# Expert steps: four turns of the gated product, in one block or among the next step's first gate products

## The chip, the cores and the metric

The kernel runs on one core of one Trainium2 chip. The metric is the device time of one execution in microseconds, the median of three runs. The times in the profile are those of one profiled execution of the same program.

## The reference

A decoder trunk of two layers on 256 tokens of width 1024, in float32. Each layer has an input projection, a windowed attention group beside a convolution group, an output projection and a feed-forward part. The feed-forward part of the first layer is dense; that of the second is a mixture of 8 experts, two for each token. The change touches the second alone:

```python
def moe_swiglu(h, w_router, w_gate, w_up, w_down):
    ...
    for e in range(N_EXPERTS):
        y = (jax.nn.silu(t @ w_gate[e]) * (t @ w_up[e])) @ w_down[e]
        out = out + combine[:, e:e + 1].astype(t.dtype) * y
    return out.reshape(B, S, D)
```

`w_gate[e]` and `w_up[e]` are 1024 x 3584, `w_down[e]` is 3584 x 1024.

## The kernel before

Every large product is made of three: each operand is split into a high part in the matmul's format and a low part (the rest), and high x high, high x low and low x high are added up in PSUM (`TERMS`, the helper `terms`). For the weights ScalarE (ACT) makes the high part (`high`, L726) and VectorE (DVE) the low part (`low`, L1035). A weight slot is 128 x 2048 values, 1 MB. The raw slots form a ring of 6, the split ones a ring of 3 (`PART_RING`), so ACT may start on a slot only when TensorE has used the slot three before it (`w_used`), and SyncE loads a raw slot when DVE is done with the slot six before it (`w_low_done`).

Each expert takes up to 128 gathered rows of tokens, and its 3584 inner columns go in 7 steps of 512: 56 steps in all (`EG` = 7). A step has six weight slots and 72 products, each with a 128 x 128 stationary operand and 512 moving columns:

- gate: 2 slots, 24 products into PSUM bank 0. Stationary is a piece of the expert's tokens (`xg`, in the profile `hT_both`), moving is the weight (`w_high` or `w_low`);
- up: 2 slots, 24 products into bank 1;
- down: 2 slots, 24 products into banks 4 and 5, stationary is the gated product's split transpose (`act_both`).

Between up and down the step's numbers go round: ACT takes silu of bank 0 (L935), DVE multiplies it by bank 1 into `prod_t` (L1378, 128 x 512, in the profile `work_a`), TensorE turns `prod_t` in four chunks of 128 columns into bank 2 (`turn_act`, L1772: four transposes against the identity, each a weight load and a 128-column matmul), ACT copies bank 2 as the high part (`act_copy`, L917), and DVE makes the low part (`act_low`, L1345).

TensorE's order is written out by hand in `expert_steps`. In round k it does gate and up of step k+1, then down of step k, then the four turns of step k+1. So a block of four turns stands between the last down product of one round and the first gate product of the next. The waits are written beside: `prod_done` ahead of the turns; `silu_done`, `prod_done`, once for each expert `xg_low_done`, and `w_low_done` of the first gate slot ahead of the first gate product. The first step is prepared ahead of the loop, with its turns between its successor's gate and up. In round 54 (`mid`) the turns of the last step stand between the two halves of down, and the last round has only down.

Two other kinds of turns stand in the stream. Once for each of the experts but the first, eight of them turn the fetched rows of the next expert (`turn_rows`, L1743) between up and down, into banks 3 and 6; and once, at `LAST_STEP`, two of them (L1823) go into bank 3.

ACT's order in a round, with t for the round's first slot, is `high(t+2)`, `act_copy`, `high(t+3)`, silu, `high(t+4)` and on; DVE's is `low(t+2)`, `act_low`, `low(t+3)` and on. `high(t+3)` waits until TensorE has used slot t, the first gate slot. Neither order is touched by the change.

Of the kernel before, what the change touches and what calls it, by code (L numbers as in the profile page):

```python
# [22 lines left out]
P = 128  # L23
# [7 lines left out]
def hybrid_trunk(nc, x, attn_norm_g, w_in, q_norm_g, k_norm_g, sinks, conv_w, conv_b, conv_ln_g,  # L31
# [43 lines left out]
    def at(i, per, const):  # L75

        return const if i is None else i * per + const

    with ExitStack() as ctx:
        def sb(name, shape, dt=F32):  # L80
            return ctx.enter_context(nc.sbuf_tensor(name, shape, dt))

        def sem(name):
            return ctx.enter_context(nc.semaphore(name))
# [18 lines left out]
        ident = sb("ident", [P, P])  # L103
# [59 lines left out]
        ps = ctx.enter_context(nc.psum_tensor("ps", [P, 8, 512], F32))  # L163
# [49 lines left out]
        prod_t = work_a[:, 2560:3072]  # L213
# [78 lines left out]
        act_turned = sem("act_turned")  # L292
# [1184 lines left out]
        def _(pe):  # L1477
            def mm(out_, lhsT, rhs, start, stop=False):
                return pe.matmul(out_, lhsT, rhs, start=start, stop=stop, skip_group_check=True)  # L1479

            def terms(out_, tokens, tidx, weights, widx, start, stop, weights_move=True):

                for n, (a, w) in enumerate(TERMS):
                    x_ = tokens[a][tidx]
                    w_ = weights[w][widx]
                    lhsT, rhs = (x_, w_) if weights_move else (w_, x_)
                    last = mm(out_, lhsT, rhs, start and n == 0, stop and n == 2)
                return last

            def slot(s, k, i=None, per=0):  # L1490
                pe.wait_ge(w_low_done, at(i, per, s + 1))
                return [part_slot(0, s, k), part_slot(1, s, k)]
# [245 lines left out]
            def turn_rows(i, per, e):  # L1738

                pe.wait_ge(rows_scaled, at(i, per, e))  # L1740
                for j in range(2):
                    for k in range(4):
                        last = pe.transpose(ps[:, (3, 6)[j], k * P:(k + 1) * P], xrows[:, (4 * j + k) * P:(4 * j + k + 1) * P], ident[:, :])  # L1743
                    last.then_inc(gathered, 1)

            def arriving_rows(j, w):

                for a, ns in ((0, range(2)), (1, range(1))):
                    for m in range(4):
                        k = BY_BANK[4 * j + m] - 4 * j  # L1750
                        pe.wait_ge((first_high_done, first_low_done)[a], 4 * j + m + 1)
                        for n in ns:
                            last = mm(ps[:, 0, :], xg[a][:, 4 * j + k, 0, :], w[n][:, k, :], (a, j, m, n) == (0, 0, 0, 0), (a, j, m) == (1, 1, 3))
                return last

            def gate_up(s, r, i, per, arriving=False, ms=range(2)):

                for m in ms:
                    for j in range(2):
                        w = slot(s + 2 * m + j, 4, i, per)  # L1760
                        if arriving and m == 0:
                            last = arriving_rows(j, w)
                            last.then_inc(w_used, 1)
                            continue
                        for k in range(4):
                            last = terms(ps[:, m, :], xg, (slice(None), 4 * j + k, r, slice(None)), w, (slice(None), k, slice(None)),
                                         j == 0 and k == 0, j == 1 and k == 3)
                        last.then_inc(w_used, 1)

            def turn_act():  # L1770
                for f in range(4):
                    last = pe.transpose(ps[:, 2, f * P:(f + 1) * P], prod_t[:, f * P:(f + 1) * P], ident[:, :])  # L1772
                last.then_inc(act_turned, 1)

            def down_and_scatter(t, a):

                def scatter(hf, b, part):

                    return mm(ps[:, 2 * hf + b, :], slot_of[:, b, :], y_part[part][:, hf * 512:(hf + 1) * 512], part == 0, part == 1)

                pe.wait_ge(slot_copied, 1)
                for j in range(2):
                    w = slot(t + j, 2)
                    for hf in range(2):
                        for f in range(2):
                            last = terms(ps[:, 4 + hf, :], a, (slice(None), 2 * j + f, slice(None)), w, (slice(None), f, slice(hf * 512, (hf + 1) * 512)),
                                         False, j == 1 and f == 1)
                        if j == 1:
                            last.then_inc(y_half, 1)
                pe.wait_ge(y_high_done, 1)  # L1790
                scatter(0, 0, 0)
                pe.wait_ge(y_low_done, 1)
                scatter(0, 0, 1).then_inc(scattered, 1)
                scatter(0, 1, 0)
                scatter(0, 1, 1).then_inc(scattered, 1)
                pe.wait_ge(y_high_done, 2)
                for b in range(NB):
                    scatter(1, b, 0)
                n_passes = passes_in_all(pe)
                pe.wait_ge(y_low_done, 2)  # L1800
                for b in range(NB):
                    scatter(1, b, 1).then_inc(scattered, 1)
                pe.sem_inc(w_used, 2)
                pe.sem_inc(y_copied, 1)
                return n_passes

            def expert_steps(s, n, e, experts, following, i, pers):

                per_s, per_n, per_e = pers
                for k in range(experts * EG):  # L1810
                    last_step = k == experts * EG - 1 and not following
                    t = s + 6 * k
                    if not last_step and (i is not None or k):
                        pe.wait_ge(silu_done, at(i, per_n, DG + n + k + 1))
                        pe.wait_ge(prod_done, at(i, per_n, DG + n + k + 1))
                        nxt = (k + 1) // EG
                        if k % EG == EG - 1:
                            pe.wait_ge(xg_low_done, at(i, 2 * per_e, 2 * (e + nxt + 1)))
                        gate_up(t, (e + nxt) % 2, i, per_s)
                        if i is None and k == LAST_STEP:  # L1820
                            pe.wait_ge(last_onehot, NB)
                            for b in range(NB):
                                last = pe.transpose(ps[:, 3, b * P:(b + 1) * P], onehot[:, b, NE - 1], ident[:, :])  # L1823
                            last.then_inc(slot_turned, 1)
                        if k % EG == GATHER_AT and (k // EG + 1 < experts or following):
                            turn_rows(i, per_e, e + k // EG + 1)
                    pe.wait_ge(act_low_done, at(i, per_n, DG + n + k + 1))
                    if k % EG == 0:
                        pe.wait_ge(y_copied, at(i, per_e, e + k // EG + 1))
                    a = [p_[:, k % 2, :].rearrange("p (f c) -> p f c", f=4) for p_ in act_part]  # L1830
                    if last_step and i is None:
                        return down_and_scatter(t, a)
                    mid = i is None and k == experts * EG - 2
                    for j in range(2):
                        w = slot(t + (0 if last_step else 4) + j, 2, i, per_s)
                        if j == 1 and mid:
                            pe.wait_ge(prod_done, at(i, per_n, DG + n + k + 2))
                            turn_act()
                        for f in range(2):
                            for hf in range(2):  # L1840
                                last = terms(ps[:, 4 + hf, :], a, (slice(None), 2 * j + f, slice(None)), w, (slice(None), f, slice(hf * 512, (hf + 1) * 512)),
                                             k % EG == 0 and j == 0 and f == 0, k % EG == EG - 1 and j == 1 and f == 1)
                        last.then_inc(w_used, 1)
                    if not last_step and not mid:
                        pe.wait_ge(prod_done, at(i, per_n, DG + n + k + 2))
                        turn_act()

# [60 lines left out]
            for k in range(4, KC):  # L1908
                last = mm(ps[:, 5, 0:NE], hT_plain[:, k, P:S], wr[:, k, 0:NE], False, k == KC - 1)
# [59 lines left out]
```

## Time and profile before

| | |
|---|---|
| median of 3 runs | 1340.37 us (1339.83 to 1340.76) |
| span of the profiled execution | 1339.4 us, granted TensorE clock 1.000 |
| TensorE matmul busy | 1330.6 us, 99% of the span |
| weight loads (beside the matmuls) | 1109.6 us, 83% |
| VectorE busy | 1126.6 us, 84% |
| ScalarE busy | 933.0 us, 70% |
| expert steps | 399.7 us to the end of the span, 56 steps |

The span runs from the first to the last instruction of the core; the run's time has 0.97 us more. A matmul's time in the trace reaches past the start of the next one, since matmuls are pipelined. What a matmul costs the stream is the distance of its start to the start of the next, and that is read from the starts in the first column of a timeline.

### The profile page before, as it was taken

The numbers are of one execution on the slowest core, as the hardware profiler recorded it, in microseconds if no ns is written. First come the engines' busy times: TensorE is split into PE (matmuls) and PEld (weight loads), VectorE is DVE, ScalarE is ACT, GpSimd is POOL, SyncE is SP. The second block draws the span as 40 slices with busy tenths as digits, with TensorE's granted clock in tenths as the row PEclk, the third lists the DMA queues.
The fourth block names the chain that finished last, engine by engine and source line by source line (L and its number), as shares of the span: only waits on it lengthen the run. The fifth ranks groups of instructions, "written<-read, shape, count | busy, mean of one in ns | idle before, by whom it ended". The sixth has DMA issues, their size and how long they took to land.

```text
span 1339.4 us, 16909 instructions
## 1 busy us (share of the span) xinstructions
PE 1330.6 (99%) x6957; PEld 1109.6 (83%) x6958; DVE 1126.6 (84%) x818; ACT 933.0 (70%) x787; POOL 130.5 (10%) x143
## 2 busy tenths in 40 slices
PE   9999999999999999999999999999999999999998
PEld 8879888898788888888888888888888888888886
DVE  6867666677678999998998889889888988988997
ACT  6675444465777777777777777777777777777774
POOL 3410000021047500000000000000000000000010
PEclk9999999999999999999999999999999999999999
DMA  9845555646369999999999999999999999999994
GB/s 308 254 160 190 189 190 190 189 154 197 130 214 370 393 390 388 394 358 375 398 382 365 390 393 376 376 387 382 366 394 394 369 374 390 390 366 369 395 395 182
DMA packets 199155, 430.79 MB, mean 322 GB/s; under 512 B 9768, under 2 KB 42816, under 8 KB 199072
## 3 DMA queue, kind: packets, MB, share of 16 engines
q1 hardware_dynamic: 193952, 415.40, 85.7%
q0 software_dynamic: 4576, 13.50, 2.7%
q8 instruction: 57, 0.93, 0.3%
q10 hardware_dynamic: 544, 0.75, 0.2%
q14 instruction: 26, 0.21, 0.0%
HBM read 417.56 MB, written 7.36 MB: 317 GB/s over the span
## 4 chain that ended last, share of the span: by engine, by line
PE 96%; DMA 1%; POOL 1%; DVE 1%; SPq 0%; ACT 0%; issue 0%; DVEq 0%; POOLq 0%
PE ps L1479 92%; PE ps L1772 2%; DMA raw<-in_w_in 1%; POOL work_b L560 1%; PE ps L1743 0%; PE ps L1505 0%; PE ps L1641 0%; DMA work_b<-in_conv_w 0%; DMA hT_both<-hpad 0%; SPq L455 0%; DVE w_low L1035 0%; DVE xr L1339 0%; ACT w_high L726 0%; PE ps L1607 0%; POOL tmp L600 0%
## 5 line engine op out<-in xcount | busy, mean ns | idle before, releaser
L1035 DVE TENSOR_TENSOR w_low<-raw,w_high 128x2048 fp32r<-128x2048 f32 x387 | 892.2, 2306 | 132.9 <-ACT w_high L726 132.5
L726 ACT ACTIVATE w_high<-raw 128x2048 fp32r<-128x2048 f32 x389 | 745.3, 1917 | 267.8 <-PE ps L1479 267.3
L1479 PE MATMUL ps<-w_high,hT_both 128*128 128x512 f32 (+1 forms) x1920 | 599.3, 389 | 0.3 <-DVE w_low L1035 0.3
L1479 PEld LDWEIGHTS ps<-w_high,hT_both 128*128 128x128 f32 x1920 | 358.8, 188 | 71.9 <-DVE w_low L1035 0.8
L1479 PE MATMUL ps<-w_low,hT_both 128*128 128x512 f32 (+1 forms) x960 | 370.7, 386 | 0.0
L1479 PE MATMUL ps<-w_high,act_both 128*128 128x512 f32 x1072 | 342.4, 391 | 0.0
L1479 PEld LDWEIGHTS ps<-w_high,act_both 128*128 128x128 f32 x1072 | 201.4, 188 | 41.5 <-issue 0.3
L1479 PEld LDWEIGHTS ps<-w_low,hT_both 128*128 128x128 f32 x960 | 180.7, 188 | 34.8
L1479 PE MATMUL ps<-w_low,act_both 128*128 128x512 f32 x536 | 208.9, 390 | 0.0
L1479 PE MATMUL ps<-hT_both,w_high 128*128 128x256 f32 (+1 forms) x640 | 140.1, 339 | 0.0
L1479 PEld LDWEIGHTS ps<-hT_both,w_high 128*128 128x128 f32 x640 | 108.9, 190 | 11.0 <-DVE hT_both L1048 0.2
L1479 PEld LDWEIGHTS ps<-w_low,act_both 128*128 128x128 f32 x536 | 100.7, 188 | 20.2
L1479 PE MATMUL ps<-hT_both,w_low 128*128 128x256 f32 x480 | 89.9, 283 | 0.0
L1479 PEld LDWEIGHTS ps<-hT_both,w_low 128*128 128x128 f32 x480 | 74.3, 191 | 3.2
L693 POOL DMA_DIRECT2D y_slots<-work_a x7 | 4.1, 591 | 711.3 <-ACT work_a L955 711.3
L935 ACT ACTIVATE work_a<-ps 128x512 f32<-128x512 f32 x55 | 33.0, 599 | 39.7 <-PE ps L1479 39.7
L1345 DVE TENSOR_TENSOR act_both<-ps,act_both 128x512 fp32r<-128x512 f32 x56 | 38.3, 684 | 0.0
L1378 DVE TENSOR_TENSOR work_a<-ps,work_a 128x512 f32<-128x512 f32 x55 | 37.6, 683 | 0.0
L917 ACT ACTIVATE act_both<-ps 128x512 fp32r<-128x512 f32 x56 | 32.4, 579 | 2.4 <-PE ps L1772 2.4
L1772 PEld LDWEIGHTS ps<-ident,work_a 128*128 128x128 f32 x224 | 27.9, 140 | 7.2
L1772 PE MATMUL ps<-ident,work_a 128*128 128x128 f32 x224 | 33.5, 272 | 0.0
L1066 DVE COPY work_a<-ps 128x512 f32<-128x512 f32 x20 | 13.8, 691 | 22.2 <-PE ps L1479 22.2
(276 smaller groups left out, 708.0 us busy)
## 6 DMA issues: line engine op xcount, KB each, us to landing
raw<-in_moe_w_gate SPq DMA_DIRECT2D x112, 1024.0 KB, 7.9
raw<-in_moe_w_up SPq DMA_DIRECT2D x112, 1024.0 KB, 7.7
raw<-in_moe_w_down SPq DMA_DIRECT2D x112, 1024.0 KB, 7.6
raw<-in_w_in SPq DMA_DIRECT2D x13, 1024.0 KB, 5.6
raw<-in_dense_w_gate SPq DMA_DIRECT2D x11, 1024.0 KB, 5.5
raw<-in_dense_w_up SPq DMA_DIRECT2D x11, 1024.0 KB, 5.3
raw<-in_dense_w_down SPq DMA_DIRECT2D x11, 1024.0 KB, 5.0
raw<-in_w_out SPq DMA_DIRECT2D x8, 1024.0 KB, 6.8
```

The lines of the kernel that those rows point to most:

```text
L560: pool.dma_start(tap_rows[CG * i:CG * (i + 1), l, 0:QUAD * n].rearrange("g (j c) -> g j c", j=n), conv_w[l, 4 * i:4 * i + n, :].rearrange( ...
L693: pool.dma_start(y_dram[bass.ds(m * P, P), :], y_sb).then_inc(y_stored, 16)
L726: act.activation(w_part[0][:, s % PART_RING, :], raw[:, s % RAW_RING, :], ACT.Copy).then_inc(w_high_done, 1)
L917: act.activation(act_part[0][:, k % 2, :], ps[:, 2, :], ACT.Copy).then_inc(act_high_done, 1)
L935: act.activation(silu_t, ps[:, 0, :], ACT.Silu).then_inc(silu_done, 1)
L1035: dve.tensor_tensor(w_part[1][:, q, :], raw[:, r, :], w_part[0][:, q, :], ALU.subtract).then_inc(w_low_done, 1)
L1066: link(dve.tensor_copy(whole, parts[:, :, 1, :]))
L1345: dve.tensor_tensor(act_part[1][:, k % 2, :], ps[:, 2, :], act_part[0][:, k % 2, :], ALU.subtract).then_inc(act_low_done, 1)
L1378: dve.tensor_tensor(prod_t, ps[:, 1, :], silu_t, ALU.mult).then_inc(prod_done, 1)
L1479: return pe.matmul(out_, lhsT, rhs, start=start, stop=stop, skip_group_check=True)
L1772: last = pe.transpose(ps[:, 2, f * P:(f + 1) * P], prod_t[:, f * P:(f + 1) * P], ident[:, :])
```

## The change

In each round from the second on (k > 0, outside the overflow passes) the four turns are not done as one block after down. They are done in the next call of `gate_up`: one turn ahead of each of the first four groups of three gate products. The first turn stands where the block's first turn stood; the other three stand 3, 6 and 9 products later. What the turn writes (bank 2) and reads (`prod_t`) is the same. The waits that stood ahead of the first gate product now stand ahead of the first turn. The end of the fourth turn counts `act_turned`, as before. The turns of the first step and those of the last (`mid`) stay as blocks. 54 of the 56 blocks are changed.

```diff
-            def gate_up(s, r, i, per, arriving=False, ms=range(2)):
+            def gate_up(s, r, i, per, arriving=False, ms=range(2), turns=False):
...
                         for k in range(4):
+                            if turns and (m, j) == (0, 0):
+                                turned_chunk = turn_chunk(k)
+                                if k == 3:
+                                    turned_chunk.then_inc(act_turned, 1)
                             last = terms(ps[:, m, :], xg, (slice(None), 4 * j + k, r, slice(None)), w, (slice(None), k, slice(None)),
                                          j == 0 and k == 0, j == 1 and k == 3)
                         last.then_inc(w_used, 1)
 
+            def turn_chunk(f):
+
+                return pe.transpose(ps[:, 2, f * P:(f + 1) * P], prod_t[:, f * P:(f + 1) * P], ident[:, :])
+
             def turn_act():
                 for f in range(4):
-                    last = pe.transpose(ps[:, 2, f * P:(f + 1) * P], prod_t[:, f * P:(f + 1) * P], ident[:, :])
+                    last = turn_chunk(f)
                 last.then_inc(act_turned, 1)
...
-                        gate_up(t, (e + nxt) % 2, i, per_s)
+                        gate_up(t, (e + nxt) % 2, i, per_s, turns=i is None and k > 0)
...
-                    if not last_step and not mid:
+                    if i is not None and not last_step:
                         pe.wait_ge(prod_done, at(i, per_n, DG + n + k + 2))
                         turn_act()
```

TensorE's order at the seam between two rounds, before: the last down products (`act_both`), the block, the first gate products (`hT_both`) of the next step.

```order
L1479 MATMUL ps<-w_low,act_both 128x512
L1479 MATMUL ps<-w_high,act_both 128x512
L1772 MATMUL ps<-ident,work_a 128x128 [waits prod_done]
L1772 MATMUL ps<-ident,work_a 128x128 x3
L1479 MATMUL ps<-w_high,hT_both 128x512 [waits w_low_done,prod_done,silu_done]
L1479 MATMUL ps<-w_low,hT_both 128x512
L1479 MATMUL ps<-w_high,hT_both 128x512 x2
```

The same place in the changed kernel, where the turn has line 1776:

```order
L1479 MATMUL ps<-w_high,act_both 128x512
L1776 MATMUL ps<-ident,work_a 128x128 [waits w_low_done,prod_done,silu_done]
L1479 MATMUL ps<-w_high,hT_both 128x512
L1479 MATMUL ps<-w_low,hT_both 128x512
L1479 MATMUL ps<-w_high,hT_both 128x512
L1776 MATMUL ps<-ident,work_a 128x128
L1479 MATMUL ps<-w_high,hT_both 128x512
L1479 MATMUL ps<-w_low,hT_both 128x512
L1479 MATMUL ps<-w_high,hT_both 128x512
L1776 MATMUL ps<-ident,work_a 128x128
```

Three turns moved down by 3, 6 and 9 products, and the first gate product's waits moved up onto the first turn. The number of matmuls and of weight loads is the same. On ACT, DVE, SyncE and GpSimd nothing moved.

## Rows read from the trace of the kernel before

**Rows 1.** The page: busy time of the engines; the chain that ended last, by engine.
```profile
PE 1330.6 (99%) x6957; PEld 1109.6 (83%) x6958; DVE 1126.6 (84%) x818; ACT 933.0 (70%) x787; POOL 130.5 (10%) x143
...
PE 96%; DMA 1%; POOL 1%; DVE 1%; SPq 0%; ACT 0%; issue 0%; DVEq 0%; POOLq 0%
```

**Rows 2.** Waits of TensorE, then SyncE, from 400 us: total, times, longest.
```profile
PE ps L1479 <- DVE hT_both L1333: 0.8, 1, 0.8
```
```profile
SPq L415 <- DVE w_low L1035: 787.2, 323, 3.7
```

**Rows 3.** TensorE's timeline in the last down: start, length, engine, line, count.
```profile
1324.44 0.39 PE L1479 MATMUL ps<-w_low,act_both 128*128 128x512 f32 x1
...
1330.56 0.39 PE L1479 MATMUL ps<-w_low,act_both 128*128 128x512 f32 x1
```

**Rows 4.** TensorE's timeline at a block of four turns.
```profile
749.78 0.39 PE L1479 MATMUL ps<-w_high,act_both 128*128 128x512 f32 x1
750.01 0.60 PE L1772 MATMUL ps<-ident,work_a 128*128 128x128 f32 x4
...
750.68 0.39 PE L1479 MATMUL ps<-w_low,hT_both 128*128 128x512 f32 x1
...
751.38 0.39 PE L1479 MATMUL ps<-w_low,hT_both 128*128 128x512 f32 x1
...
753.44 0.39 PE L1479 MATMUL ps<-w_low,hT_both 128*128 128x512 f32 x1
```

**Rows 5.** Chain that ended last: start and length of the products between blocks.
```profile
733.82 16.36 PE ps L1479 x72
750.61 16.37 PE ps L1479 x72
767.42 16.36 PE ps L1479 x72
...
818.75 16.37 PE ps L1479 x72
```

**Rows 6.** TensorE's timeline at the block of two turns.
```profile
1234.99 0.39 PE L1479 MATMUL ps<-w_low,hT_both 128*128 128x512 f32 x1
...
1235.44 0.38 PE L1823 MATMUL ps<-ident,work_b 128*128 128x128 f32 x2
...
1237.26 0.39 PE L1479 MATMUL ps<-w_low,act_both 128*128 128x512 f32 x1
```

**Rows 7.** TensorE's timeline, last row ahead of and a later one behind eight turns.
```profile
455.79 0.39 PE L1479 MATMUL ps<-w_low,hT_both 128*128 128x512 f32 x1
...
458.05 0.39 PE L1479 MATMUL ps<-w_low,act_both 128*128 128x512 f32 x1
```

**Rows 8.** The page's costliest groups: the turn's matmul, with its mean length.
```profile
L1772 PE MATMUL ps<-ident,work_a 128*128 128x128 f32 x224 | 33.5, 272 | 0.0
```

**Rows 9.** Weight loads' timeline: the first two behind the block of 766.82 us.
```profile
767.15 0.19 PEld L1479 LDWEIGHTS ps<-w_high,hT_both 128*128 128x128 f32 x1
767.26 0.19 PEld L1479 LDWEIGHTS ps<-w_low,hT_both 128*128 128x128 f32 x1
```

**Rows 10.** TensorE's timeline: products of 256 columns, then of 512.
```profile
199.36 1.11 PE L1479 MATMUL ps<-hT_both,w_low 128*128 128x256 f32 x8
200.32 2.00 PE L1479 MATMUL ps<-hT_both,w_high 128*128 128x512 f32 x8
```

**Rows 11.** ScalarE's timeline after the block at 766.82 us.
```profile
768.90 0.58 ACT L917 ACTIVATE act_both<-ps 128x512 fp32r<-128x512 f32 x1
770.27 1.92 ACT L726 ACTIVATE w_high<-raw 128x2048 fp32r<-128x2048 f32 x1 [0.79 <-PE ps L1479]
```

**Rows 12.** VectorE's timeline: act_low and low(t+3) of that round; then at 815 us.
```profile
771.24 0.68 DVE L1345 TENSOR_TENSOR act_both<-ps,act_both 128x512 fp32r<-128x512 f32 x1
772.22 2.29 DVE L1035 TENSOR_TENSOR w_low<-raw,w_high 128x2048 fp32r<-128x2048 f32 x1 [0.30 <-ACT w_high L726]
```
```profile
815.33 4.59 DVE L1035 TENSOR_TENSOR w_low<-raw,w_high 128x2048 fp32r<-128x2048 f32 x2
```

## The prediction

> **What bounds the kernel now.** First the page: TensorE is busy for 99% of the span, at a mean granted clock of 1.000 (the table above), and the chain that ended last is 96% TensorE [rows 1]. Then the waits: from 400 us on TensorE waits once, for 0.8 us, in the last step [rows 2]. So in the expert steps the time is the sum of the distances from one matmul's start to the next, and nothing else; a change pays or costs there only by what it does to these distances, or by bringing in a wait. The other engines wait for TensorE: SyncE spends 787.2 us until DVE gives a slot back, and ACT in turn stands idle until TensorE has used a slot [rows 2, 11].
>
> Then the timeline of TensorE, for the price of each kind. From 1324.44 to 1330.56 us, in undisturbed products, there are 27 of them: 6.12 / 27 = **0.2267 us** a product [rows 3]. A block of turns is priced by taking the products out of a stretch that has it in the middle:
> - four turns: from 749.78 to 753.44 us are 14 products and the block, 3.66 - 14 x 0.2267 = 0.49 us [rows 4]. Over whole steps: the chain's groups of 72 products start 16.79 and 16.81 us apart, less 72 x 0.2267 = 16.32 leaves 0.47 and 0.49 [rows 5]. The two values alternate from step to step; mean **0.48**, 0.12 a turn;
> - two turns: 1234.99 to 1237.26 us, 9 products, 2.27 - 2.04 = 0.23 (0.22 to 0.23 with the rounding) [rows 6];
> - eight turns: 455.79 to 458.05 us, 6 products, 2.26 - 1.36 = 0.90 [rows 7].
>
> **What a block consists of.** Four turns last 0.60 us together and one lasts 0.272, so inside a block they start (0.60 - 0.272) / 3 = 0.109 us apart [rows 4, 8]. Of the block of four, 4 x 0.109 = 0.44 are turns, and the other 0.03 to 0.05 lie around it: a little at the two edges, and in the first products behind it. After the block three products take 751.38 - 750.68 = 0.70 us, where 0.68 is the undisturbed value [rows 3, 4]. I call that the echo. It is not bound to the turns: it also stands after a run of 256-column products, where the eight products behind start (2.00 - 0.39) / 7 = 0.230 us apart instead of 0.227 (0.39 is one product's length, [rows 3]) [rows 10]. Behind the block of two there is hardly any: 0.23 - 2 x 0.109 = 0.01 for both edges and all that follows [rows 6].
>
> **The change, part by part.**
>
> 1. *Four turns alone instead of four in a row, 54 times.* No matmul and no weight load is added or taken away. What counts is the price of a turn with 512-column products on both sides, which no row shows. The nearest row is the block of two: take out one inner distance, 0.227 - 0.109 = 0.118 us for one turn with both its edges. Four of them cost 0.47 us, against 0.48 for the block: 0.008 x 54 = **-0.4 us** with 0.479 for the mean block. That is my value.
> Bound below: a lone turn cannot be cheaper than a turn inside a block, 0.109, if the load is what spaces them. The weight loads show that it is: behind the block that starts at 767.42 - 0.60 = 766.82 us [rows 4, 5] the fourth turn starts 3 x 0.109 later, at 767.15; the first gate product's load starts at that time and the next load 0.11 us later, the spacing of the turns themselves [rows 9]. In the new order a turn's own load hides under a product, but the load of the product behind it can start only when the turn has its weights, and stands open beside a short matmul. So of each load that is newly hidden one is newly open: four open loads per block before (three turns and the first product), four after (the products behind the turns). 4 x 0.109 = 0.44, saved 0.04 x 54 = 2.3 us.
> Bound above: each lone turn brings the edges and the echo of a whole block. Three products behind a block take 0.02 more [rows 3, 4], so 0.118 + 0.016 four times, and the rest of an echo of about 0.02 at the end: 0.55 us, 0.07 more than now, x 54 = +3.8 us.
> I take the value next to the block of two, because it is the shortest block there is and shows no echo.
>
> 2. *A change of PSUM bank in an open group.* Turns write bank 2 while bank 0 is being added up. Down alternates between banks 4 and 5 with every three products, and [rows 3] is down: no price shows. Nothing for this.
>
> 3. *The waits moved up by a block.* The first turn now also waits for the low part of the first gate slot, and at an expert's start for the tokens' low parts. The least slack is in the rounds that follow a block of eight turns: DVE makes the low parts of both gate slots in one row from 815.33, 4.59 us for two, so the first ends near 817.6 [rows 12]; the block stands 0.60 ahead of the chain's next group, at 818.75 - 0.60 = 818.15 [rows 5], 0.5 us later. `silu_done` and `prod_done` were due at the same place before. Queued behind the wait is all of TensorE's work, so what exceeds the slack would be paid in full, to the chain. Zero.
>
> 4. *`act_turned` comes later.* Before, the fourth turn starts 3 x 0.109 = 0.33 after the first and ends at 0.60. Now it starts after 9 products and 3 turns, 9 x 0.2267 + 3 x 0.118 = 2.39, and ends at 2.67 us. ACT copies at 768.90, that is 2.08 after the first turn [rows 11], since `high(t+2)` is ahead of it in its queue; it will start near 2.7 and end near 3.3. Behind it in ACT's queue is `high(t+3)`, which starts at 770.27, or 3.45, and is held by TensorE's use of slot t (idle 0.79 ahead of it, released by PE) [rows 11]. Slot t is used after 12 products and 4 turns as before, so this start stays and the copy fits in the idle time with 0.15 to 0.25 us left. DVE's `act_low` is at 771.24, 4.42 after the turn, so it is not reached either [rows 12]. If the cover were gone, `high(t+3)` would slip, and behind it `low(t+3)`, which ends at 774.51; TensorE wants slot t+3 after 36 products, 766.82 + 0.48 + 36 x 0.2267 = 775.46: another 0.95 us. Zero.
>
> 5. *The ends.* `prod_t` and bank 2 are written again some 12 us later. Round 54 and the first step stay. Zero.
>
> **Sum**: 1340.37 - 0.4 = **1340.0 us** (the profiled execution: 1339.4 - 0.4 = 1339.0, and 0.97 around it). A measurement of this kernel can tell about 0.2% (2.7 us) from no change, so this is "the same".
>
> **Rivals.**
>
> *A. Each turn has an echo* (slower). Mechanism: what slows the products behind a run of short matmuls does so behind every single one, at four places in each step. Against it: the block of two shows none. For it: the block of four has as much as the block of eight has (0.90 - 8 x 0.109 = 0.03), so it is not simply in proportion to the number of turns, and the 256-column runs show that it hangs on the change of pace. It gives 1340.4 + 3.8 = 1344.2. It decides (over 0.2%) from 0.05 us a step on, that is from 0.132 us a lone turn.
>
> *B. The load behind a lone turn hides too* (faster). If TensorE had taken the next product's weights ahead while the long product still ran, a lone turn would cost only its columns. A product of 512 columns costs 0.227 [rows 3], one of 256 costs (200.32 - 199.36) / 8 = 0.120 [rows 10]; by the difference 128 columns fewer save 0.053, and a turn costs 0.067. With the edges of 0.01, 4 x 0.077 = 0.31, 0.17 saved x 54 = -9.2 us, 1331.2. Against it: each load starts with the matmul ahead of it, never earlier [rows 4, 9], and the last turn of a block, which already has a product behind it, is not cheaper than the others. The transfers would have to come 1% sooner, which the 787.2 us that SyncE waits for slots leave room for [rows 2].
> The Trainium skill, "TensorE: Matmul & The Clock Gate", section "Step-by-step: what each phase is for", says that TensorE can pull weight loads ahead of matmuls in flight when they go to the background buffer. Read as one load ahead it is what the loads behind the block show and gives no gain; read as several ahead it gives rival B. The same page's section "Wait — 56ns, not 53.3ns?" has 56 ns for a warm 128-column matmul; by that figure, as an estimate, B would save 0.255 x 54 = 13.8 us. No row here shows a 128-column matmul so cheap; its section "LDWEIGHTS (loading the stationary operand)" has columns / 1.2 ns, 107 for 128, with which the 0.109 agrees.
>
> *C. Edges and echo vanish* (faster, by too little to be told): the lower bound of part 1, 0.44 a step, 1340.4 - 2.3 = 1338.1.
>
> *D. The change does nothing to the stream*: exactly the same price as a block; that lies within the forecast.
>
> **How the numbers follow.** Forecast with D (from -1 to +1.5 us): 0.60. C (down to -2.5): 0.13. A: 0.17, nearly all of it over +2.7 us. B: 0.07. Left over, a wait that I have not seen: 0.03, slower. Faster by over 0.2%: B and the far edge of C, 0.09. Slower: A and the rest, 0.19. Within 0.2%: 0.72. The range takes in C and A and leaves out B and the unseen wait: 1337.7 to 1344.3.
>
> **What would show it.** In the timeline after, a turn and its three products should take 0.118 + 0.680 = 0.80 us, and the starts of two rounds' first turns lie 16.80 us apart as before; 0.76 would be B, 0.81 to 0.82 A. ACT's copy should start about 2.7 us after the first turn, with the next `high` still released by TensorE at 3.45; a release by ACT's own copy, or a wait of TensorE for `w_low`, would refute part 4 or 3. The page's busy times of ACT and DVE should not move, and the clock should stay. The prediction is wrong if the price of a lone turn lies outside 0.109 to 0.134 us.

## The result

| | before | changed |
|---|---|---|
| median | 1341.29 us (10 runs, 1339.83 to 1342.25) | 1344.38 us (10 runs, 1343.77 to 1345.73) |
| span of the profiled execution | 1339.4 us | 1342.7 us |

The ratio is 1.0027, 95% interval 1.0018 to 1.0035: the change makes the kernel slower by 3.1 us in the medians and 3.3 us in the two traces. The forecast was no change.

The page of the changed kernel, busy time of the engines and ScalarE's group of the turned product's copy (the last columns are busy time, mean ns, and the idle time ahead with who ended it):

```profile
PE 1334.0 (99%) x6957; PEld 1102.5 (82%) x6958; DVE 1126.5 (84%) x818; ACT 938.9 (70%) x787; POOL 126.9 (9%) x143
...
L917 ACT ACTIVATE act_both<-ps 128x512 fp32r<-128x512 f32 x56 | 33.4, 597 | 28.9 <-PE ps L1776 28.9
```

TensorE is still busy 99% of the span [rows 1], DVE did the same work in the same time. Before, the copy of the turned product waited 2.4 us in total for its turns; now it waits 28.9 us for the fourth turn. Two stretches of the trace, split at the first block of turns: first before, then changed (stretch, its length, busy PE, PEld, DVE, ACT, POOL, clock, DMA share, GB/s):

```profile
399.72:1339.40 939.68, 933.68 (x4251) 772.72 (x4249) 841.80 (x480) 697.38 (x463) 71.14 (x54) 1.00 1.01 375
```
```profile
399.41:1342.70 943.29, 937.58 (x4251) 765.75 (x4249) 841.91 (x480) 703.36 (x463) 67.53 (x54) 1.00 1.00 373
```

The whole loss is in the expert steps: 943.29 - 939.68 = 3.6 us, 0.067 us for each of the 54 changed rounds, at the same clock. And it is no wait. TensorE's waits from 400 us on are still this single one, as in [rows 2]:

```profile
PE ps L1479 <- DVE hT_both L1333: 0.8, 1, 0.8
```

So the products themselves got slower. TensorE's timeline of the changed kernel at one round's seam, which answers to [rows 4]:

```profile
784.89 0.27 PE L1776 MATMUL ps<-ident,work_a 128*128 128x128 f32 x1
...
785.69 0.27 PE L1776 MATMUL ps<-ident,work_a 128*128 128x128 f32 x1
...
786.52 0.27 PE L1776 MATMUL ps<-ident,work_a 128*128 128x128 f32 x1
...
787.33 0.27 PE L1776 MATMUL ps<-ident,work_a 128*128 128x128 f32 x1
787.36 0.49 PE L1479 MATMUL ps<-w_high,hT_both 128*128 128x512 f32 x1
...
789.75 0.39 PE L1479 MATMUL ps<-w_low,hT_both 128*128 128x512 f32 x1
```

The record of the product behind a turn starts only 0.03 us after the turn's (787.36 and 787.33) and is longer than others, so single distances mean nothing there; only whole stretches do. A turn and its three products take 0.80, 0.83 and 0.81 us, where three undisturbed products take 0.68. The fourth turn and the ten products up to 789.75 take 2.42 - 10 x 0.2267 = 0.15 more than the products alone. In sum 0.12 + 0.15 + 0.13 + 0.15 = 0.55 us for what cost 0.47 to 0.49 as a block [rows 4, 5]. The chain shows the same over a whole round, from first turn to first turn, 801.93 - 785.05 = 16.88 us against 16.80. This is one of the longer rounds: the 45 rounds that hold no other turns take 16.82 to 16.88, 16.867 in the mean, against 16.800 before. That is 0.547 us for four lone turns against 0.480 for the block, the 0.067 from above.

```profile
785.05 0.11 PE ps L1776
...
801.93 0.11 PE ps L1776
```

What the loads do at the seam shows in the weight loads' timeline of the changed kernel:

```profile
784.66 0.14 PEld L1776 LDWEIGHTS ps<-ident,work_a 128*128 128x128 f32 x1
784.89 0.19 PEld L1479 LDWEIGHTS ps<-w_high,hT_both 128*128 128x128 f32 x1
785.00 0.19 PEld L1479 LDWEIGHTS ps<-w_low,hT_both 128*128 128x128 f32 x1
```

The turn's own load (784.66) now runs beside the long product ahead of it. The load of the product behind the turn starts with the turn, at 784.89, and the next load 0.11 us later, as behind a block [rows 9]. No load of the expert steps, before or after, starts earlier than the matmul ahead of it.

### The profile page after: what moved, and what is told of

Read it like the earlier page. It is cut to its first block, busy times and chain, and to the rows that moved or that the text cites. A ratio compares the mean times of both kernels' runs of the same rounds, so it can differ in the third digit from the quotient of the medians.

```text
span 1342.7 us, 16909 instructions
## 1 busy us (share of the span) xinstructions
PE 1334.0 (99%) x6957; PEld 1102.5 (82%) x6958; DVE 1126.5 (84%) x818; ACT 938.9 (70%) x787; POOL 126.9 (9%) x143
## 4 chain that ended last, share of the span: by engine, by line
PE 97%; DMA 1%; POOL 1%; DVE 0%; ACT 0%; issue 0%; SPq 0%; DVEq 0%; POOLq 0%
PE ps L1479 93%; PE ps L1776 2%; DMA raw<-in_w_in 1%; POOL work_b L560 1%; PE ps L1743 0%; PE ps L1505 0%; PE ps L1641 0%; DMA work_b<-in_conv_w 0%; DVE w_low L1035 0%; DVE xr L1339 0%; ACT w_high L726 0%; PE ps L1607 0%; POOL tmp L600 0%; ACT L818 0%; POOL h_rows L680 0%
## 5 line engine op out<-in xcount | busy, mean ns | idle before, releaser
L1479 PE MATMUL ps<-w_high,hT_both 128*128 128x512 f32 (+1 forms) x1920 | 619.5, 397 | 0.4 <-DVE w_low L1035 0.4
L1776 PE MATMUL ps<-ident,work_a 128*128 128x128 f32 x224 | 59.8, 271 | 0.0
L917 ACT ACTIVATE act_both<-ps 128x512 fp32r<-128x512 f32 x56 | 33.4, 597 | 28.9 <-PE ps L1776 28.9
L1776 PEld LDWEIGHTS ps<-ident,work_a 128*128 128x128 f32 x224 | 31.3, 140 | 9.7
```

What stands on the lines that cost most here:

```text
L917: act.activation(act_part[0][:, k % 2, :], ps[:, 2, :], ACT.Copy).then_inc(act_high_done, 1)
L1776: return pe.transpose(ps[:, 2, f * P:(f + 1) * P], prod_t[:, f * P:(f + 1) * P], ident[:, :])
```

## The experiments

The question is why a lone turn costs 0.12 to 0.15 us when half of a pair costs 0.113. All kernels differ from the one before or the changed one at the seam of 54 rounds only (where an expectation says 53, it is 54 too). I read from each how long a round lasts, from a seam to the next, in rounds without the expert's ends; 72 products alone are 16.32 us. The times of single executions stand beside those of the kernel before on the same chip: 1340.70 (first four) and 1341.02 us (next four), one execution each, and 1340.90 us (the others, median of 15). A kernel's executions differ by 2 us and more, so what a turn costs is read from the rounds, not from these times.

### Leaving turns out: none, one, two in a row

```diff
-                            if turns and (m, j) == (0, 0):
-                                turned_chunk = turn_chunk(k)
-                                if k == 3:
-                                    turned_chunk.then_inc(act_turned, 1)
...
+                            if turns and (m, j, k) == (0, 0, 0):
+                                last.then_inc(act_turned, 1)
```

> The turns of 54 rounds are left out; what ScalarE and VectorE copy is then not the turned product. Everything else stands as in the changed kernel. If the slower products around the turns are caused by the turns (the theory of the echo), the first gate products go at 0.227 us like all others and a round takes 72 x 0.2267 = 16.32 us, so that the turns with all they bring are worth 16.87 - 16.32 = 0.55 us a round in the changed kernel and 0.48 in the one before. If instead the first gate products are slow by themselves (the rival: what ScalarE, VectorE or the transfers do at that time), part of the excess stays and a round takes 16.34 to 16.40.

Measured 1317.06 us. TensorE's timeline, the first gate products of two rounds that follow each other:

```profile
708.87 0.39 PE L1479 MATMUL ps<-w_high,hT_both 128*128 128x512 f32 x1
...
725.19 0.39 PE L1479 MATMUL ps<-w_high,hT_both 128*128 128x512 f32 x1
```

16.32 us: without turns the first gate products are as fast as all others. Nothing that ACT, DVE or the transfers do there slows them; the excess belongs to the turns. The time fell by 23.6 us and not by 54 x 0.48 = 25.9. Part of the rest (7 x 0.18 us) lies in the rounds behind an expert's end, where ACT copies the expert's result ahead of the slots' high parts. Without the turns' time these slots seem not to be ready soon enough: VectorE ends the low part of the first up slot at 516.11 us, and the product that needs it was due at 516.20. TensorE loses a moment there, and once more at the next slot, in the middle of plain products (the profile's list of waits does not have it, so the cause of the pause is argued):

```profile
515.06 0.39 PE L1479 MATMUL ps<-w_low,hT_both 128*128 128x512 f32 x1
...
515.74 0.39 PE L1479 MATMUL ps<-w_low,hT_both 128*128 128x512 f32 x1
...
516.50 0.40 PE L1479 MATMUL ps<-w_low,hT_both 128*128 128x512 f32 x1
...
517.19 0.39 PE L1479 MATMUL ps<-w_low,hT_both 128*128 128x512 f32 x1
...
517.87 0.39 PE L1479 MATMUL ps<-w_low,hT_both 128*128 128x512 f32 x1
```

Three products take 0.68, then 0.76 with the pause, then 0.69, and only then 0.68 again. Slower products also follow a pause, with no turn near. So it takes neither a turn nor its data to make them slow.

```diff
-                        turn_act()
+                        turn_act(range(1) if i is None else range(4))
```

(`turn_act` takes the chunks to turn; in the other kernel it is `range(2)`.)

> Of the block of four turns before the first gate product only the first turn is done, in 53 rounds; the other three are left out. Echo theory (each lone turn brings 0.118 us and slows the products behind it): 0.12 to 0.16 us over 16.32 a round, with products of 0.230 to 0.237 us behind the turn. Rival (a lone turn has no echo and the changed kernel's loss comes from where its turns stand): 0.118, with products of 0.227 from the second one on.

> Only the first two of the four turns of the block are done, in 53 rounds; two are left out. This is the block of two whose price the prediction took from the one at the last expert step, where identity-like data are turned. If the number of turns decides and two in a row have no echo: 0.227 us over 16.32 a round, as there. If a pair of the real product has an echo like the block of four: 0.25 to 0.28.

Measured 1322.16 and 1328.21 us. The chain of the kernel with one turn, then of that with two:

```profile
693.88 0.11 PE ps L1772
693.99 16.34 PE ps L1479 x72
710.33 0.11 PE ps L1772
```
```profile
696.44 0.22 PE ps L1772 x2
...
712.99 0.22 PE ps L1772 x2
```

One turn: 710.33 - 693.88 = 16.45, or 16.447 over more rounds, **0.127** over 16.32. Two: 712.99 - 696.44 = 16.55, **0.227**. So the first turn costs 0.13 and the second only 0.10, less than its own distance of 0.109. The pair of the real product costs what the pair of [rows 6] did, so what those data were played no part. The timelines show where it lies: behind the single turn the products from 694.06 us on take 0.69, behind the pair those from 696.73 on take 0.68 at once.

```profile
694.06 0.40 PE L1479 MATMUL ps<-w_low,hT_both 128*128 128x512 f32 x1
...
694.75 0.39 PE L1479 MATMUL ps<-w_low,hT_both 128*128 128x512 f32 x1
```
```profile
696.73 0.39 PE L1479 MATMUL ps<-w_low,hT_both 128*128 128x512 f32 x1
...
697.41 0.39 PE L1479 MATMUL ps<-w_low,hT_both 128*128 128x512 f32 x1
```

The rival of a lone turn without an echo has fallen, and a new theory was set up to be tried: **pace**. The stream of products has a fixed pace of 0.2267 us. Two turns with their edges last just that; the products behind them are in step at once. One turn does not, nor does a pause, and the stream runs slower until it has found its pace.

### The waits moved, the turns not

```diff
-                            if turns and (m, j) == (0, 0):
-                                turned_chunk = turn_chunk(k)
-                                if k == 3:
-                                    turned_chunk.then_inc(act_turned, 1)
+                            if turns and (m, j) == (0, 0) and k == 0:
+                                turn_act()
```

> The block of four stays a block, but stands behind the waits of the next step's first gate slot, as the first lone turn does in the changed kernel. If the moved waits or the one more semaphore instruction of TensorE cost time, a round takes more than the 16.80 us of before. The prediction's part 3 says nothing is lost: 16.80, and the same alternation of 0.47 and 0.485.

Measured 1340.36 us against 1340.70. The chain has the kernel before's two values again, 16.79 and 16.81 us from block to block:

```profile
699.64 0.44 PE ps L1774 x4
...
716.43 0.43 PE ps L1774 x4
...
733.24 0.44 PE ps L1774 x4
```

The moved waits cost nothing. The loss is the spreading alone: this kernel and the changed one have the same waits at the same place, and differ in where three of the turns stand.

### The distance between two lone turns, and two pairs

```diff
-                            if turns and (m, j) == (0, 0):
+                            if turns and (m, j) == (0, 0) and k in (0, 1):
                                 turned_chunk = turn_chunk(k)
-                                if k == 3:
+                                if k == 1:
```

(In the other kernel it is `k in (0, 2)`, and `k == 2`.)

> Only two of the four turns are done, in 54 rounds, each alone, with three gate products between them; two are left out. In one row these two cost 0.2267 us. If each lone turn is a disturbance of its own: 2 x 0.1267 = 0.253 us at least, more if the second comes before the products have found back to 0.227 (0.26 to 0.28), a round of 16.573 to 16.60. If only the number of turns counted: 16.547.

> The same two lone turns with six products between them. If the products find back to 0.227 within three, as behind the single turn: 2 x 0.1267 = 0.253 us, a round of 16.573, whatever the distance. If the distance counts, this round is shorter than with a distance of three.

Measured 1330.64 and 1330.18 us. The chain of the first, then of the second, at the products between the two turns of a round:

```profile
696.80 0.69 PE ps L1479 x3
...
713.42 0.69 PE ps L1479 x3
```
```profile
697.63 1.38 PE ps L1479 x6
...
714.20 1.38 PE ps L1479 x6
```

Three products apart a round takes 16.62, or 0.30 for two turns; six apart 16.57, or 0.253, exactly twice the price of one. So a lone turn costs 0.127 when the stream is in step, and more when it comes while the products behind the last one are still finding back. At a distance of three, the changed kernel's, they are. Both are above the 0.227 of two in a row. The first came out above the 0.28 expected as its upper end.

```diff
-                            if turns and (m, j) == (0, 0):
-                                turned_chunk = turn_chunk(k)
-                                if k == 3:
+                            if turns and (m, j) == (0, 0) and k < 2:
+                                for f in (2 * k, 2 * k + 1):
+                                    turned_chunk = turn_chunk(f)
+                                if k == 1:
```

> As in the changed kernel, but the four turns go in two pairs, ahead of the first and of the second group of three gate products. Theory of the pace (two turns take just the time of one product, 0.2267 us, and leave the stream undisturbed, as two turns alone did): 2 x 0.227 = 0.453 us over 16.32, a round of 16.773, shorter than the 16.80 of before, and products of 0.226 to 0.227 behind each pair. Rival (every run of short matmuls costs its edges and an echo, so what counts is the number of runs): 0.50 to 0.52, a round of 16.82 to 16.84.

> The same two pairs with six gate products between them instead of three. Pace: 16.773 again, since a pair leaves nothing behind that the distance could change. Rival (an echo that needs products to die away): shorter than with a distance of three, 16.79 to 16.82.

Measured 1338.68 and 1339.91 us against 1341.02. TensorE's timeline of the first:

```profile
698.80 0.38 PE L1777 MATMUL ps<-ident,work_a 128*128 128x128 f32 x2
...
699.71 0.38 PE L1777 MATMUL ps<-ident,work_a 128*128 128x128 f32 x2
...
700.16 0.39 PE L1479 MATMUL ps<-w_low,hT_both 128*128 128x512 f32 x1
...
700.84 0.39 PE L1479 MATMUL ps<-w_low,hT_both 128*128 128x512 f32 x1
```

A pair and three products take 0.91, that is 4 x 0.2267, and three products behind the second pair take 0.68: no echo. The chain of the first, then of the second, at the products between a round's two pairs:

```profile
715.96 0.69 PE ps L1479 x3
...
732.73 0.69 PE ps L1479 x3
```
```profile
716.37 1.37 PE ps L1479 x6
...
733.15 1.37 PE ps L1479 x6
```

A round lasts 16.77 and 16.78 us by these rows and 16.773 over more rounds of each, 0.453 over the products, for either distance, as the theory of the pace had it. This is the cheapest arrangement of four turns that was run: two pairs are cheaper than four in a row (0.47 or 0.49), which are cheaper than four alone (0.55).

### Time or number

Is it that two turns last a product's time, or just that they are two?

```diff
-                            if turns and (m, j) == (0, 0):
-                                turned_chunk = turn_chunk(k)
-                                if k == 3:
-                                    turned_chunk.then_inc(act_turned, 1)
+                            if turns and (m, j, k) == (0, 0, 0):
+                                for f in range(2):
+                                    last = mm(ps[:, 7, 0:256], xg[0][:, f, r, :], w[0][:, f, 0:256], True, True)
+                                last.then_inc(act_turned, 1)
```

(In the second kernel 128 stands for 256. In the third, three turns are done in that place.)

> The same with two products of 256 columns each, 0.120 us apart in the trace of before, so that the two last 0.240 to 0.25 us: again two short ones, but not a whole product's time. All four turns are left out. Theory of the pace: slower products follow, and the cost is 0.26 us or more. Rival (two short matmuls in a row are harmless whatever they last): 0.24 to 0.25 with products of 0.227 from the second on.

> In place of the turns stand two ordinary products of 128 columns (stationary the expert's tokens, moving the split weight, into an unused bank), in 54 rounds; all four turns are left out. They should be spaced by their weight loads like turns. Theory of the pace: 0.227 us and nothing behind them, since only the time matters. Rival (it is something of the turns, their float32 identity or their data): another cost, or slower products behind.

> Three turns in one row, in 54 rounds; the fourth is left out. A run of n turns lasts, without what it leaves behind, about 0.118 + 0.109 (n - 1): 0.118, 0.227, 0.336, 0.445. Theory of the pace (quiet only when the run lasts a whole number of products' times, 0.2267, as two do): three are not quiet, slower products follow, and the cost is 0.34 to 0.37. Rival (what counts is whether the number of short matmuls is one or large; two and three are harmless): 0.336 with products of 0.227 behind it.

Measured 1328.39, 1327.58 and 1334.78 us. TensorE's timelines, one round of the kernel with 256 columns, then of that with 128 (the row of three holds the first gate product too), and the chain of the one with three turns:

```profile
712.28 0.63 PE L1479 MATMUL ps<-w_high,hT_both 128*128 128x256 f32 x3
...
728.86 0.63 PE L1479 MATMUL ps<-w_high,hT_both 128*128 128x256 f32 x3
```
```profile
711.60 0.62 PE L1479 MATMUL ps<-w_high,hT_both 128*128 128x128 f32 x3
...
728.16 0.62 PE L1479 MATMUL ps<-w_high,hT_both 128*128 128x128 f32 x3
```
```profile
697.63 0.33 PE ps L1776 x3
...
714.33 0.33 PE ps L1776 x3
```

The products behind them, with 256 columns and then with 128:

```profile
696.16 0.40 PE L1479 MATMUL ps<-w_low,hT_both 128*128 128x512 f32 x1
...
696.86 0.39 PE L1479 MATMUL ps<-w_low,hT_both 128*128 128x512 f32 x1
```
```profile
695.51 0.39 PE L1479 MATMUL ps<-w_low,hT_both 128*128 128x512 f32 x1
...
696.19 0.39 PE L1479 MATMUL ps<-w_low,hT_both 128*128 128x512 f32 x1
```

Two products of 256 columns cost 0.26 (728.86 - 712.28 = 16.58), and slower products follow them: three take 0.70, where they take 0.68 behind two of 128 columns. Two of 128 columns cost 0.233 (0.24 by the two rows shown). They are ordinary products, with other data and another format, and cost nearly a pair of turns' 0.227. Three turns cost 0.38, of which 0.336 are the turns by the reckoning of the expectation: again a tail. So number alone does not decide, and neither does the kind. The 0.38 is a little more than the 0.34 to 0.37 that I had given.

These three runs came out on the side of the pace, but one row on record speaks against it as a rule. By the same reckoning four turns in a row last 0.118 + 3 x 0.109 = 0.445 us, 0.01 us short of two products' 0.453. That is about as near as the pair of 128 columns (0.233) comes to one product. They should be quiet, and they are not: they cost 0.47 or 0.49, and three products behind them take 0.70 [rows 4, 5]. What is shown is that a run of two short matmuls that costs 0.227 or 0.233 us leaves the next products at 0.68 for three, and that every other run tried in these rounds slows them. Why is not shown.

### The pairs, timed

> The kernel of e5_pairs_3 again, timed against the kernel before. Its rounds took 16.773 us in the trace, against a mean of 16.80 before. Theory of the pace: 0.0267 us x 54 = 1.4 us faster, ratio 0.9989, and 3.7 to 4.9 us faster than the changed kernel. Rival (the trace's gain is given back elsewhere, or lies within what runs differ by): ratio 0.9995 to 1.0005.

1339.06 us (11 runs) against 1340.90 (15 runs), ratio 0.9988, 95% interval 0.9979 to 0.9997. The version with two pairs is faster than the kernel before, by little: 1.8 us, where 54 x 0.0267 = 1.4 was expected. The changed kernel was not timed beside it; its median of another occasion, 1344.38 us, is 5.3 us longer.

## Why the prediction was wrong

**What bounds the kernel**: right. The change worked only through the distances between matmuls; no wait came or went.

**Part 1, the price of a lone turn, is the step that failed.** The prediction took the block of two, 0.227, and subtracted one inner distance of 0.109, as if what remained were the edges of any run. The run with one turn has it directly: 0.127 in a stream that is in step, not 0.118, and 0.12 to 0.15 in the changed kernel, 0.137 in the mean, where the next turn comes before the stream has found back. The prediction had named a price outside 0.109 to 0.134 as the sign of being wrong. What it left out of its own sum is the echo, 0.01 us behind a turn in step and more behind turns three products apart: 4 x 0.118 = 0.47 us a round were forecast, and 0.547 came. I had chosen the row because it is "the shortest block there is and shows no echo". It does not show none because it is short: one turn is shorter and has an echo. A row that looked like the cleanest was a special case. That it is special because 0.227 is also a product's time fits the pairs and is not shown, for the block of four speaks against it. The bound below held: no turn came under 0.109. The bound above, 0.55 us for four, is the mean that was measured, and the longest rounds lie a little over it (0.56).

**Rival A** was right: products slow down behind every single turn, at four places in each step, +3.8 us for the rounds, measured 3.6 in the trace. It did not have that the price hangs on the distance between the turns. I gave it 0.17. The sign that spoke for it stood in the prediction, the slower products behind a run of 256 columns [rows 10], and that block of four and block of eight had tails of like size [rows 4, 7] (the 0.90 for eight turns stopped inside the tail; over whole rounds of that trace they cost 0.92 in the mean); against both stood one row, the pair. The range ended at 1344.3 and the median is 1344.38; the kernel before, measured ten times, also came out at 1341.29 instead of 1340.37, so against it the change is +3.1 us. Part of this stood in the prediction's base: it took the run's time as 0.97 us over the span, a median set against the span of another execution. Where both are of one execution, it is 1.5 to 1.6 us (1344.24 and 1342.7; 1341.02 and 1339.4).

**Rival B** fell: a turn with three products takes 0.80 to 0.83 us, not 0.76. The load of the product behind a lone turn stays open: it starts with the turn, at 784.89 us, and not beside the long product before. The Trainium skill's rule that weight loads are pulled ahead of matmuls in flight ("TensorE: Matmul & The Clock Gate", "Step-by-step: what each phase is for") holds only as one load ahead here.

**Rival C**, the edges gone, did not come in this kernel; the two pairs come near it with 0.453 against its 0.44.

**Part 2**, the bank change: two pairs among the gate products leave them at 0.227, so it is free there, as assumed. **Part 3**: right, by the kernel with the waits moved alone (16.79 and 16.81 us). **Part 4**: right. ScalarE's timeline of the changed kernel, behind the first turn at 784.89:

```profile
787.64 0.60 ACT L917 ACTIVATE act_both<-ps 128x512 fp32r<-128x512 f32 x1 [0.57 <-PE ps L1776]
788.40 1.93 ACT L726 ACTIVATE w_high<-raw 128x2048 fp32r<-128x2048 f32 x1 [0.16 <-PE ps L1479]
```

The copy starts 2.75 us after the first turn (forecast near 2.7). The `high` behind it starts at 3.51, still released by TensorE, with 0.16 us left of the 0.79 [rows 11]: the forecast was 0.15 to 0.25.

## What to carry to other kernels

In a stream of equal matmuls that never waits, price a foreign matmul by the whole stretch until the products behind it are at full pace again, not by its own distance. Spreading short matmuls one by one between long ones saved nothing here: each hides its own load and opens that of the product behind it, and the products behind each are slower once more. Where they must stand there, try them in pairs, which were the cheapest of the groups run here (0.453 us for four turns, against 0.47 or 0.49 in one block and 0.55 alone), and take a round's length from the trace before and after, over enough rounds to see whether it alternates. And when one clean row stands against others that show a cost, ask what is special about it before it carries the forecast: here the pair alone was quiet, and its neighbours of one, three and four were not.

## What the runs showed of the hardware

- Products with 512 moving columns, each with its own weights, follow each other every 0.2267 us. Behind a run of shorter matmuls (one, three, four or eight turns, two or many of 256 columns) or a pause of 0.08 us, three of the next products take 0.69 to 0.70 and more instead of 0.68, until the pace is back. Behind two turns they take 0.68 at once.
- What a run of turns costs is not in proportion: 0.127, 0.227, 0.380, and 0.47 or 0.49 us for one, two, three and four. Two pairs cost 0.453. Lone turns cost 0.253 for two that stand six products apart, and 0.300 for two that stand three apart.
- In the expert steps of both kernels a weight load starts with the matmul ahead of it or later, never earlier. Behind a 128-column matmul loads follow each other 0.11 us apart (784.89 and 785.00), and that is also the distance of turns inside a block.
- The four-turn block's two prices alternate from round to round in the kernel before, though some sixty products at full pace lie between two blocks; with pairs the alternation is gone. Why the stream settles as it does, after three products behind one turn and after up to ten behind three or four, no run here shows. That the pace comes from how weight loads and products meet is a guess, and it stays open.
